# Third-condition slabs ahead of the output weights, memory's value weights ahead of the first condition, columns turned inside the strips

## The reference, cut to what matters

```
c_act = silu(c)
cond  = c_act @ ada_w + ada_b            # six pieces of 1024
shift1, scale1, gate1, shift2, scale2, gate2 = split(cond)
h = rmsnorm(x, norm1_g) * (1 + scale1) + shift1
u, v, val, gate = split(h @ w_in + b_in)
y = concat(rmsnorm(gmlp(gelu(u), gelu(v))), rmsnorm(conv_mixer(val, gate)))
x = x + gate1 * (y @ w_out)
h2 = rmsnorm(x, norm2_g) * (1 + scale2) + shift2
x = x + gate2 * (swiglu(h2 @ w_ffn_in) @ w_ffn_out)
x = rmsnorm(x, norm_f_g) * (1 + scale_f) + shift_f      # c_act @ ada_f_w
```

## Time and profile before

| what | value |
|---|---|
| median of 3 runs | 746.39 us (745.61 to 747.97) |
| the profiled execution, its own time | 747.3 us |
| span of that execution in the trace | 745.5 us |
| mean granted TensorE clock | 0.981 |
| busy PE / DVE / ACT / POOL | 93% / 48% / 43% / 9% |
| bytes moved | 211.42 MB, mean 284 GB/s |

### The profile page before, as it was taken

How to read it: one execution, slowest core, us unless ns; L and a number is a source line. 1 busy time by engine, 2 the same in 40 slices (tenths; PEclk the granted TensorE clock), 3 DMA queues, 4 the chain that set the end, 5 groups by cost and what they waited for, 6 DMA issues and landing times.

```text
span 745.5 us, 12984 instructions
## 1 busy us (share of the span) xinstructions
PE 691.8 (93%) x5377; PEld 543.0 (73%) x5378; DVE 361.1 (48%) x718; ACT 323.5 (43%) x685; POOL 68.1 (9%) x76
## 2 busy tenths in 40 slices
PE   5989998999999999999999899997999999978886
PEld 4677694879999999999878778786765555534352
DVE  4557997457544545444788797335521111001111
ACT  6355546437444333334678896666411111101001
POOL 0400002020000002000200036450000000000000
PEclk9999999999999999999999999999999999989999
DMA  9997959659666545555664356659879999999995
GB/s 341 382 368 300 418 218 329 249 169 378 222 238 230 177 170 171 177 170 176 199 200 130 112 180 190 239 193 404 337 309 422 421 420 421 421 421 420 421 405 199
DMA packets 76706, 211.42 MB, mean 284 GB/s; under 512 B 7463, under 2 KB 34245, under 8 KB 62822
## 3 DMA queue, kind: packets, MB, share of 16 engines
q1 hardware_dynamic: 75602, 209.91, 74.8%
q0 software_dynamic: 800, 0.63, 0.6%
q10 hardware_dynamic: 244, 0.03, 0.0%
HBM read 209.51 MB, written 1.05 MB: 282 GB/s over the span
## 4 chain that ended last, share of the span: by engine, by line
PE 69%; DMA 12%; SPq 6%; DVE 6%; ACT 5%; issue 2%; POOL 1%; ACTq 0%; DVEq 0%; POOLq 0%
PE ps L1988 10%; PE ps L1989 9%; PE ps L1990 9%; SPq L462 6%; PE ps L2001 5%; PE ps L2718 5%; PE ps L2002 5%; PE ps L2003 5%; DMA ring<-in_expert_w_down_dram 5%; DMA ring<-in_expert_w_gate_dram 4%; DMA ring<-in_ada_w_dram 3%; PE ps L2683 3%; PE ps L2760 2%; PE ps L2069 2%; DVE ring_low L1240 2%; PE ps L2211 2%
## 5 line engine op out<-in xcount | busy, mean ns | idle before, releaser
L1240 DVE TENSOR_TENSOR ring_low<-ring,HI 128x1024 fp32r<-128x1024 f32 (+1 forms) x119 | 140.2, 1221 | 16.6 <-ACT HI L729 16.6
L729 ACT ACTIVATE HI<-ring 128x1024 fp32r<-128x1024 f32 (+1 forms) x135 | 133.5, 1055 | 22.2 <-DMA ring<-in_w_in_dram 20.2
L1988 PE MATMUL ps<-AH,HI 128*128 128x256 f32 (+1 forms) x328 | 92.3, 282 | 1.0 <-DVE Z L1504 0.6
L1990 PE MATMUL ps<-AH,ring_low 128*128 128x256 f32 (+1 forms) x328 | 91.8, 280 | 0.0
L1989 PE MATMUL ps<-AL,HI 128*128 128x256 f32 (+1 forms) x328 | 91.7, 280 | 0.0
L2718 PE MATMUL ps<-ring,ZM 128*32 128x256 f32 x880 | 69.3, 409 | 11.6 <-DMA ring<-in_expert_w_up_dram 7.9
L1988 PE MATMUL ps<-HI,AH 128*128 128x512 f32 x160 | 65.3, 408 | 1.7 <-DVE AH L1756 0.6
L1988 PEld LDWEIGHTS ps<-AH,HI 128*128 128x128 f32 (+1 forms) x328 | 61.2, 187 | 4.0 <-issue 3.2
L1989 PE MATMUL ps<-ring_low,AH 128*128 128x512 f32 x160 | 62.8, 393 | 0.0
L1989 PEld LDWEIGHTS ps<-AL,HI 128*128 128x128 f32 (+1 forms) x328 | 61.4, 187 | 0.0
L1990 PEld LDWEIGHTS ps<-AH,ring_low 128*128 128x128 f32 (+1 forms) x328 | 61.2, 187 | 0.0
(11 more groups left out here) (395 smaller groups left out, 1265.5 us busy)
## 6 DMA issues: line engine op xcount, KB each, us to landing
ring<-in_expert_w_up_dram SPq DMA_DIRECT2D x28, 1024.0 KB, 22.8
ring<-in_expert_w_gate_dram SPq DMA_DIRECT2D x27, 1024.0 KB, 26.2
ring<-in_expert_w_down_dram SPq DMA_DIRECT2D x24, 1024.0 KB, 22.7
ring<-in_w_ffn_in_dram SPq DMA_DIRECT2D x20, 1024.0 KB, 5.8
ring<-in_w_in_dram SPq DMA_DIRECT2D x18, 1024.0 KB, 6.1
ring<-in_ada_w_dram SPq DMA_DIRECT2D x16, 1024.0 KB, 9.9
ring<-in_w_ffn_out_dram SPq DMA_DIRECT2D x11, 1024.0 KB, 7.2
ring<-in_ada_w_dram SPq DMA_DIRECT2D x16, 512.0 KB, 12.0
```

The source lines that it names most:

```text
L729: act(HI[:, (i + 1) % UNITS, 0:w], W.view(name)[:, o:o + w], ACT.Copy).then_inc(s_hi, 1)
L1240: tt(W.low(name)[:, o:o + w], W.view(name)[:, o:o + w], HI[:, (i + 1) % UNITS, 0:w].bitcast(F32), ALU.subtract).then_inc(s_lo, 1)
L1988: mm(dst, lh, rh, start=start, stop=False)
L1990: return mm(dst, ll, rh, start=False, stop=stop)
```

## The change

The loads in SP's program: `kv_v1` goes ahead of all four slabs `ada00` to `ada03`; `in_g1` goes ahead of the spatial weights `wsv`; `in_w1` goes ahead of `ada14`; `ada24` to `ada27` go ahead of `out1` to `out3` and take slots 7, 4, 5 and 0 (behind `in_u1`, `in_w0`, `in_w1` and `ada20`), and `out1` to `out3` take slots 1, 2 and 3 (behind `ada21` to `ada23`). The order of slots after that is renamed in the same way, [7, 4, 5, 0, 6, 1, 2, 3] for [0, 1, 2, 3, 6, 7, 4, 5].

PE: the row constants `rows1` are turned ahead of mem; the slabs of the first half stand behind the second and third kv unit, its columns are turned within the fourth; the second half's columns are turned within the second unit of `in_g0`; `in_v1` stands ahead of the transposes of `wsv`.

ACT and DVE: mem's scaled tiles come ahead of mem's statistics; `lower_half(1)` takes the remainder of unit 8 (the first of `in_v1`) ahead of `colv`; the split of `out1`'s first unit leaves the stretch of the taps on both engines (`iw + 5` for `iw + 3 + AHEAD`), and is done behind the group roots, which on ACT now come ahead of the output weights' units.

```diff
--- before.py
+++ after.py
@@ -497,32 +497,30 @@
                 const(MX[t], A["mem_2"].rearrange("o (t p) d -> p (o t) d", p=P)[:, t, :], s_mem)
             W.apart("ada", 4)
             rows128("kv_v0", w_kv, 512, 512, 0, 4)
-            ada_half(0, (0, 1))
             rows128("kv_v1", w_kv, 512, 512, 4, 4)
-            ada_half(0, (2, 3))
+            ada_half(0, (0, 1, 2, 3))
             rows128("in_v0", w_in, 1024, 512, 0, 4)
             ada_half(1, (0, 1))
             rows128("in_g0", w_in, 1536, 512, 0, 4)
             ada_half(1, (2, 3))
             rows128("in_v1", w_in, 1024, 512, 4, 4)
+            rows128("in_g1", w_in, 1536, 512, 4, 4)
             const(wsv, A["a_spatial_w"].rearrange("o h t s -> t (o h) s"), s_ws)
-            rows128("in_g1", w_in, 1536, 512, 4, 4)
             sp.dma_start(brow_v, A["b_in"][:, 512:1024]).then_inc(*W.other(BROW))
             rows128("in_u0", w_in, 512, 512, 0, 4)
             ada(A["ada_w"], 1, (0, 1), 2048)
             rows128("in_u1", w_in, 512, 512, 4, 4)
             ada(A["ada_w"], 1, (2, 3), 2048)
             rows128("in_w0", w_in, 0, 512, 0, 4)
-            ada(A["ada_w"], 1, (4,), 2048)
             rows128("in_w1", w_in, 0, 512, 4, 4)
-            ada(A["ada_w"], 1, (5, 6, 7), 2048)
+            ada(A["ada_w"], 1, (4, 5, 6, 7), 2048)
             rows128("out0", w_out, 0, D, 0, 2)
             ada(A["ada_w"], 2, (0, 1, 2, 3), 4096)
             W.together([7, 4, 5, 0, 1, 2, 3])
+            ada(A["ada_w"], 2, (4, 5, 6, 7), 4096)
             for h in range(1, 4):
                 rows128(f"out{h}", w_out, 0, D, 2 * h, 2)
-            ada(A["ada_w"], 2, (4, 5, 6, 7), 4096)
-            W.together([0, 1, 2, 3, 6, 7, 4, 5])
+            W.together([7, 4, 5, 0, 6, 1, 2, 3])
             ada(A["ada_f_w"], 3, range(5), 0)
             for i in range(NPAIR):
                 if i == 0:
@@ -781,6 +779,15 @@
             ac.wait_ge(s_sqs, SQ_X + 2)
             act(RTS[0], RTS[0], ACT.Sqrt, scale=1.0 / D, bias=eps[:, 0:1]).then_inc(s_rn, 1)
 
+            ac.wait_ge(s_rc, 1)
+            for kk in range(4):
+                ac.wait_ge(s_mtp, kk + 1)
+                for k in (2 * kk, 2 * kk + 1):
+                    ins = act(MH[:, k, :], ps[MTB[kk]][:, 256 * (k % 2):256 * (k % 2) + 256], ACT.Copy,
+                              scale=C1[:, NM + k:NM + k + 1])
+                ins.then_inc(s_mh, 1)
+                if kk < 2:
+                    hi_to(kk)
             for t in range(NT):
                 if t:
                     ac.wait_ge(s_mn, 1)
@@ -789,16 +796,6 @@
                 act(JM, MX[t], ACT.Square, accum_out=mst[:, t:t + 1]).then_inc(s_mn, 1)
             ac.wait_ge(s_mn, 2)
             act(mst[:, 4:6], mst[:, 0:2], ACT.Sqrt, scale=1.0 / D, bias=eps[:, 0:1]).then_inc(s_mn, 1)
-            hi_to(0)
-            ac.wait_ge(s_rc, 1)
-            for kk in range(4):
-                ac.wait_ge(s_mtp, kk + 1)
-                for k in (2 * kk, 2 * kk + 1):
-                    ins = act(MH[:, k, :], ps[MTB[kk]][:, 256 * (k % 2):256 * (k % 2) + 256], ACT.Copy,
-                              scale=C1[:, NM + k:NM + k + 1])
-                ins.then_inc(s_mh, 1)
-                if kk == 0:
-                    hi_to(1)
             hi_to(3)
 
             def upper_half(h):
@@ -866,7 +863,7 @@
             diagonals(4)
             hi_to(iw + 2 + AHEAD)
             diagonals(5)
-            hi_to(iw + 3 + AHEAD)
+            hi_to(iw + 5)
             diagonals(6)
             ac.wait_ge(s_un, S.end["in_w1"])
             for ct in range(4):
@@ -889,11 +886,10 @@
             for k in range(4):
                 ac.wait_ge(s_yt, k + 1)
                 act(AH[:, k, :], YA[:, k, :], ACT.Copy).then_inc(s_ah, 1)
-            for i in (0, 1):
-                hi_to(io + i + AHEAD)
             rooted(RGS, ps[3][:, 0:16], SUM_G)
             warm(ACT.Silu)
-            hi_to(io + 2 + AHEAD)
+            for i in (0, 1, 2):
+                hi_to(io + i + AHEAD)
             for h in range(2):
                 ac.wait_ge(s_gn, h + 3)
                 for ct in (2 * h, 2 * h + 1):
@@ -1285,20 +1281,19 @@
             for kk in range(4):
                 ve.wait_ge(s_xp, kk + 1)
                 copy(XC[:, 2 * kk:2 * kk + 2, :], tiles(ps[kk][:, :], 2)).then_inc(s_xc, 1)
-            recip(RTS[0], SUM_X)
-            ve.wait_ge(s_mn, 3)
-            ve.reciprocal(mst[:, 4:6], mst[:, 4:6]).then_inc(s_mn, 1)
             ve.wait_ge(s_rp, 1)
             copy(C1[:, 0:ROWS1], ps[5][:, 0:ROWS1]).then_inc(s_rc, 1)
-            lo_to(0)
+            recip(RTS[0], SUM_X)
             for kk in range(4):
                 ve.wait_ge(s_mh, kk + 1)
                 for k in (2 * kk, 2 * kk + 1):
                     ins = stt(ML[:, k, :], ps[MTB[kk]][:, 256 * (k % 2):256 * (k % 2) + 256], C1[:, NM + k:NM + k + 1],
                               MH[:, k, :].bitcast(F32), ALU.mult, ALU.subtract)
                 ins.then_inc(s_ml, 1)
-                if kk == 0:
-                    lo_to(1)
+                if kk < 2:
+                    lo_to(kk)
+            ve.wait_ge(s_mn, 3)
+            ve.reciprocal(mst[:, 4:6], mst[:, 4:6]).then_inc(s_mn, 1)
             ve.wait_ge(s_rb, RB_X)
             ve.wait_ge(s_xc, 4)
             for kk in range(4):
@@ -1316,6 +1311,8 @@
                 if h:
                     ve.wait_ge(s_cnp, 1)
                 copy(CN[:, 0, 0:256], ps[7][:, 0:256]).then_inc(s_cn, 1)
+                if h:
+                    lo_to(8)
                 ve.wait_ge(s_cnp, h + 1)
                 ve.wait_ge(s_rc, 1)
                 tt(half(colv[:, 0, :])[:, :, h], ps[7][:, 0:256].rearrange("p (x s c t) -> p s c x t", x=2, s=2, c=2)[:, :, :, :, 0],
@@ -1404,7 +1401,7 @@
             taps(20, 22)
             lo_to(iw + 2 + AHEAD)
             taps(22, 26)
-            lo_to(iw + 3 + AHEAD)
+            lo_to(iw + 5)
             taps(26, 29)
 
             io = S.first["out0"]
@@ -2005,7 +2002,7 @@
             def tile_of(banks, m):
                 return ps[banks[m // 2]][:, 256 * (m % 2):256 * (m % 2) + 256]
 
-            def strip(names, banks, op, k0, bias=None, between=None, lh=None, ll=None, per=1, low=None):
+            def strip(names, banks, op, k0, bias=None, between=None, lh=None, ll=None, per=1, low=None, within=None):
 
                 us = [u for n in names for u in range(S.first[n], S.end[n])]
                 if bias is not None:
@@ -2028,6 +2025,8 @@
                                         h, l, k == 0 and bias is None, i == len(us) - 1 and j == 1)
                         if i == len(us) - 1 and t == 0:
                             ins.then_inc(s_t0, 1)
+                        if within is not None:
+                            within(i, t)
                     ins.then_inc(s_un, 1)
                     if between is not None:
                         between(i)
@@ -2120,7 +2119,8 @@
                         ins = tr(ps[kk][:, 256 * (k % 2) + P * t:256 * (k % 2) + P * t + P], X[:, t, by128(k)], ident[:, :])
                 ins.then_inc(s_xp, 1)
             te.wait_ge(s_set, MATS)
-            te.wait_ge(s_cr, 2)
+            te.wait_ge(s_r1, 16 * LOADS1)
+            tr(ps[5][:, 0:ROWS1], rows1[0:ROWS1, :], ident[0:ROWS1, 0:ROWS1]).then_inc(s_rp, 1)
             te.wait_ge(s_mem, 32)
             for kk in range(4):
                 te.wait_ge(s_xc, kk + 1)
@@ -2128,18 +2128,20 @@
                     for t in range(NT):
                         ins = tr(ps[MTB[kk]][:, 256 * (k % 2) + P * t:256 * (k % 2) + P * t + P], MX[t][:, by128(k)], ident[:, :])
                 ins.then_inc(s_mtp, 1)
-            te.wait_ge(s_r1, 16 * LOADS1)
-            tr(ps[5][:, 0:ROWS1], rows1[0:ROWS1, :], ident[0:ROWS1, 0:ROWS1]).then_inc(s_rp, 1)
+            te.wait_ge(s_cr, 2)
             spread(4, 256, 0, SUM_X)
 
             def between_kv(i):
-                if i < 2:
-                    ada_half(0, 2 * i)
-                    ada_half(0, 2 * i + 1)
-                if i == 2:
+                if 0 < i < 3:
+                    ada_half(0, 2 * i - 2)
+                    ada_half(0, 2 * i - 1)
+
+            def within_kv(i, t):
+                if i == 3 and t == 0:
                     columns_half(0)
 
-            strip(("kv_v0", "kv_v1"), VMB, 0, 0, None, between_kv, MH, ML, low=s_ml)
+            te.wait_ge(s_rc, 1)
+            strip(("kv_v0", "kv_v1"), VMB, 0, 0, None, between_kv, MH, ML, low=s_ml, within=within_kv)
 
             def by_channel(names, place, n, starts, between, q0=0):
 
@@ -2155,6 +2157,8 @@
                             ins = halves(place(ct), h, l, AH[:, k, :], AL[:, k, :], k == 0 and ct in starts, k == 7)
                         if n == "gate" and q == 3 and ct < 3:
                             ins.then_inc(s_glu, 1)
+                        if n == "gate" and q == 1 and ct == 0:
+                            columns_half(1)
                     ins.then_inc(s_un, 1)
                     between(q)
 
```

(3 more changed lines are left out.)

## The result

The change takes 741.69 us (median of 6 runs, 740.17 to 742.87); the kernel before, on the same chip, 746.76 us (745.43 to 747.97). The ratio is 0.9922, its 95% interval 0.9893 to 0.9951: faster by 0.8%. The forecast was 740.9 in 738.2 to 744.0. The profiled execution took 741.83 us, its span is 740.1 us (745.5 before), its mean granted clock 0.984 (0.981). In the prediction two group numbers are interchanged: SP's queue is group 5 and the stretches are group 4.

What follows compares the result with a forecast made beforehand. PE was taken as busy 93% of the span, losing time to late slabs and a lowered clock, DVE's taps and the start's loads. 0.7 lost against 1.1, 4.3 and 0.8 won gave 5.5 us: 740.9 us, range 738.2 to 744.0.

Steps and rivals of the forecast that it cites:

- The slabs: Third pass: ada24 to ada27 land earlier, so the projection begins at 127.4, not 132.08; 4.3 us and 0.8 us won.
- the waits: PE's waits for the late slabs ada25 to ada27 ahead of the projection disappear; 4.3 us won.
- the clock: If the clock does not fall, nine projection passes ahead of the spread take 0.12 us, not 0.21; 0.8 us won.
- The taps: DVE's taps, whose end releases PE's group means, end earlier without out1's remainder among them; 1.1 us won.
- PE is not late for it: its four slabs from 113.52 used to be followed by a wait: Claim that PE can use all of the taps' earlier end, 1.1 us.
- The start: Up to in_g1's end: 1.25 us won at in_v1, 1.4 lost to transposes, 0.6 to the mask; 0.7 lost with rounding.
- the ten transposes: Moved from PE's wait to behind in_v1, they cost 1.4 us on PE's path.
- the mask's collision: POOL's mask of the spatial weights shuts out DVE's AL and remainders near 51.8 us; 0.6 us lost.
- my bound: Start's worst end: spatial weights land at 59.0, mask ends at 60.1, transposes cost 2.4 us more; 3.1 us lost.
- as argued: Every gain reaches the end one for one, since the transfer-bound last stretch starts earlier and keeps its length.
- the clock's fall: Rival: clock falls all the same on the projection, costing 1.5 us (742.4), at worst 3.0 (743.9); chance 0.15.
- the rest: Other rivals: start wins, 739.0, chance 0.12; slabs no earlier, 746.0, 0.08; slower as ACT waits on output weights, 748.9, 0.05.

Runs made afterwards that it cites:

- late_alone: Kernel before with only the third-condition part: ada24 to ada27 loaded ahead of out1 to out3, out1's split out of the taps; 742.10 us, ratio 0.9929.
- start_alone: The change without its third-condition part, leaving only the start's edits; 746.90 us, ratio 0.9993 against the kernel before.
- taps_alone: Kernel before with only the late part's ACT and DVE edits, out1's split out of the taps, loads in old order; 747.16 us, ratio 0.9996.
- busy_gap: The change with twenty transposes of the identity, computing nothing, in PE's gap ahead of in_v1; 740.52 us, ratio 0.9909 against the kernel before.
- no_mask: The change with POOL's causal mask of the spatial weights replaced by a fill of two elements; 742.19 us.

## Why the prediction was right, step by step

**The slabs: right in place, mechanism and sum; the sum is shared out wrongly.** Forecast 4.3 us for the waits and 0.8 for the clock; measured 4.44 and 0.74. late_alone shows both without the start's part, start_alone loses both without the late one. But some 1.0 of the 4.44 is clock too: before, the last slab takes 1.87 us, from its start at 130.21 to the projection at 132.08, where I reckoned with 0.91 at full clock. So the waits were worth some 3.5 and the clock some 1.7. The two go together: between 125 and 137 us the three kernels that wait for slabs (before, start_alone, taps_alone) have stretches at 1.2 GHz, and none of the eleven other profiles has one. The lateness itself I read only in part from the queue's order: the last output weight was issued by 111.61 (91.05 and 20.56), and the first slab at 114.64, once PE had read `ada20` out of the slot. The load that landed last began at 117.22, when PE was done with `ada23` (113.52 and 3.64). The order counts because it hands out the slots. The projection came at 127.92 and not at 127.4 because PE reached `ada25` at 125.21 and not at 124.6 (start and taps, below), not because of a load.

**The taps: too large by a quarter, and over another wait than I named.** Forecast 1.1. DVE's last taps after are (the first row has the 19 taps inside the view's window)

```profile
106.67 7.61 DVE L1363 SCALAR_TENSOR_TENSOR YT<-SR,cw,YT 128x256 f32<-128x256 f32 x19
...
116.96 2.46 DVE L1363 SCALAR_TENSOR_TENSOR YT<-SR,cw,YT 128x256 f32<-128x256 f32 x6
```

and end at 119.42; before it was 119.46. DVE won 1.1 us and lost as much to the later start. But PE's group means followed only at 120.08. The step that failed is "PE is not late for it: its four slabs from 113.52 used to be followed by a wait". The wait was shorter than 1.1, and it was not for the taps. PE's timeline before:

```profile
117.94 2.02 PE L2101 MATMUL ps<-ones,Z 128*128 128x128 f32 x16 [0.78 <-ACT Z L884]
119.80 1.88 PE L2255 MATMUL ps<-YT,QT 128*128 128x512 f32 x4
```

Behind the slabs PE waited 0.78 us for ACT's squares of `Z`, and DVE makes that `Z` behind the taps from which the remainder was taken. The group means then followed PE's own sums of squares, 1.86 us after their start before and 1.89 after (118.19 to 120.08), with no idle time between; the last taps don't show as what released them, though I read it so from the earlier trace rows. After, PE has no wait there: from the ones' sums to the sums of squares it took 53.87 us before and 53.02 after, 53.0 to 53.1 in the other profiles without a stretch at 1.2 GHz on that way, and 53.0 in late_alone less its stretch (54.61 less 1.6). PE's own work ended last, and the term is 0.8.

**The start: the forecast of 0.7 lost came near the 1.1 measured, by luck.** `in_v1` began at 51.10 (forecast 51.3), the ten transposes cost 1.0 (58.35 to 59.35) where I gave 1.4, and the mask's collision is real: with the clock full and the mask winning, busy_gap's ones' sums are 0.55 behind those of before, close to 0.7. But in the change's own two profiles the mask decided next to nothing: no_mask, whose clock fell there too, has its ones' sums 0.11 and 0.16 earlier. What failed is the step that let PE run at full speed behind its wait; in place of 0.6 for the mask stand 1.4 for the clock. I also let only DVE wait for the mask; in start_alone and in the change's second profile the mask waited for DVE. By moving the transposes out of the gap, the change left PE idle for 2.27 us in one piece, and the clock fell behind it in three of the four profiles with that gap (the change twice, no_mask; not start_alone), at 1.4 us each (65.22 less 63.79). The kernel before, late_alone and taps_alone have the transposes in the gap and two shorter waits around eight of them, 0.92 and 1.26 us in the kernel before; of these three the clock fell in one, late_alone. It fell in none of the other seven profiles, which have work in the gap as well and in which PE idled 1.7 us in all or less. So work in the gap alone does not keep the clock up; whether the work or the shorter idle time does it in the seven, the runs don't separate. These counts are small, and the runs don't show what decides a single execution. What the fill is worth by itself, busy_gap's 740.52 against the change's 741.69 and 742.79, is within what the intervals leave open.

Against my bound: the transposes had no 2.4 us to wait for a late load, but in start_alone the mask ended at 57.05, just as they were due (57.11). So that bound was near, by another way than I had thought.

**The sum.** Forecast 5.5 = -0.7 + 1.1 + 4.3 + 0.8; measured to the spread 4.90 = -1.10 + 0.82 + 4.44 + 0.74. All of it reached the expert loads (4.89 at 458 us), as argued; behind them the last stretch added half a microsecond whose cause is open. Of the rivals, the clock's fall did come, but at the start and not on the projection; from 125 to 130 us it is full in the change, and the rest did not occur. Without the start's part the change would be as fast (742.10), and with the start done otherwise some 4 us faster.
